# Sliding-window attention of a two-layer hybrid block: from token-major to feature-major output

## The reference

```python
scores = einsum('bnqhgd,bnkhd->bnhgqk', qb, k_ctx) * (A_HEAD_DIM ** -0.5)   # blocks of 128 queries
logits = where(valid, scores + bias, -inf)                                   # 128 or 256 keys per block
m = maximum(max(logits, axis=-1), sink)
p = exp(logits - m[..., None])
denom = sum(p, axis=-1) + exp(sink - m)
out = einsum('bnhgqk,bnkhd->bnqhgd', p / denom[..., None], v_ctx)            # S x 1024, 64 per head
...
y = sigmoid(ga) * (hm @ w_branch_m) + sigmoid(gb) * (ha @ w_branch_a)        # ha is out
```

## Time and profile before

| | |
|---|---|
| median of three executions | 2336.69 us |
| profiled execution | 2337.24 us, of which 2335.5 us are the span |
| TensorE matmul busy | 2273.0 us (97%) |
| VectorE, ScalarE, GpSimd busy | 921.2, 974.2, 886.1 us |
| mean granted TensorE clock | 0.990 of full speed |

### The profile page before, as it was taken

One profiled execution on the slowest core, in us unless ns is written; L12 is line 12 of the kernel. 1 busy time (PEld: TensorE's weight loads), 2 busy tenths in 40 slices (PEclk: granted clock), 3 DMA queues, 4 the chain that ended last, 5 costly groups with the idle time before them and its releaser, 6 DMA issues.

```text
span 2335.5 us, 35652 instructions
## 1 busy us (share of the span) xinstructions
PE 2273.0 (97%) x11333; PEld 1897.7 (81%) x11333; DVE 921.2 (39%) x1901; ACT 974.2 (42%) x2062; POOL 886.1 (38%) x672
## 2 busy tenths in 40 slices
PE   7999999999999999999999999999999999999996
PEld 5888888788888888888888788888888878888885
DVE  7344343423232235343343423232235535555452
ACT  5445455433232234455455434232235245445442
POOL 3332333445444444333323345444444231221213
PEclk9999999999999999999999999999999999999998
DMA  3221221223322222221212223323222320211112
GB/s 125 82 82 63 81 77 66 80 91 108 99 91 99 99 90 87 86 80 63 90 63 75 70 99 104 99 94 99 99 90 92 128 90 29 72 63 41 67 36 72
DMA packets 58793, 193.84 MB, mean 83 GB/s; under 512 B 6654, under 2 KB 11311, under 8 KB 58352
## 3 DMA queue, kind: packets, MB, share of 16 engines
q1 hardware_dynamic: 50400, 177.48, 22.5%
q10 hardware_dynamic: 8336, 15.60, 1.9%
HBM read 190.89 MB, written 2.16 MB: 83 GB/s over the span
## 4 chain that ended last, share of the span: by engine, by line
PE 92%; DVE 4%; ACT 2%; issue 1%; ACTq 0%; DVEq 0%; POOL 0%; POOLq 0%
PE ps L486 25%; PE ps L488 25%; PE ps L487 25%; PE ps L548 5%; PE ps L528 3%; PE ps L536 3%; PE ps L647 1%; PE ps L502 1%; PE ps L635 1%; PE ps L752 1%; PE ps L813 1%; DVE nt L1469 0%; PE ps L802 0%; PE ps L625 0%; DVE sz L1401 0%
## 5 line engine op out<-in xcount | busy, mean ns | idle before, releaser
L447 POOL TENSOR_TENSOR w_lo<-w_raw,w_hi 128x512 fp32r<-128x512 f32 x664 | 879.6, 1328 | 1428.7 <-ACT w_hi L863 1424.9
L486 PE MATMUL ps<-hT_hi,w_hi 128*128 128x512 f32 x1600 | 650.6, 407 | 2.5 <-DVE x2v L1361 2.0
L488 PE MATMUL ps<-hT_hi,w_lo 128*128 128x512 f32 x1600 | 628.1, 393 | 0.0
L487 PE MATMUL ps<-hT_lo,w_hi 128*128 128x512 f32 x1600 | 626.2, 391 | 0.0
L863 ACT ACTIVATE w_hi<-w_raw 128x512 fp32r<-128x512 f32 x664 | 411.4, 626 | 476.4 <-PE ps L488 446.8
L486 PEld LDWEIGHTS ps<-hT_hi,w_hi 128*128 128x128 f32 x1600 | 302.9, 189 | 65.8 <-issue 8.3
L488 PEld LDWEIGHTS ps<-hT_hi,w_lo 128*128 128x128 f32 x1600 | 301.8, 189 | 66.0
L487 PEld LDWEIGHTS ps<-hT_lo,w_hi 128*128 128x128 f32 x1600 | 303.0, 189 | 55.7 <-issue 0.5
L486 PE MATMUL ps<-u_hi,w_hi 128*128 128x512 f32 x512 | 199.2, 389 | 0.0
L487 PE MATMUL ps<-u_lo,w_hi 128*128 128x512 f32 x512 | 199.2, 389 | 0.0
L488 PE MATMUL ps<-u_hi,w_lo 128*128 128x512 f32 x512 | 199.2, 389 | 0.0
(11 more groups left out here) (289 smaller groups left out, 3269.7 us busy)
## 6 DMA issues: line engine op xcount, KB each, us to landing
w_raw<-w_all SPq DMA_DIRECT2D x332, 512.0 KB, 3.2
bias<-scr_w ACTq DMA_DIRECT2D x8, 512.0 KB, 3.8
biasn<-scr_n ACTq DMA_DIRECT2D x4, 1024.0 KB, 5.2
w1k<-w_in ACTq DMA_DIRECT2D x2, 1024.0 KB, 7.7
w1v<-w_in ACTq DMA_DIRECT2D x1, 2048.0 KB, 13.7
out<-x SPq DMA_DIRECT2D x8, 256.0 KB, 2.0
x<-x_in SPq DMA_DIRECT2D x4, 256.0 KB, 6.1
x<-x_in ACTq DMA_DIRECT2D x4, 256.0 KB, 5.7
```

Source lines behind the costliest of these rows:

```text
L447: nc.gpsimd.tensor_tensor(w_lo[:, h, :], raw[:, h // 2, (h % 2) * HALF:(h % 2 + 1) * HALF], w_hi[:, h, :].bitcast(F32), ALU.subtract).then ...
L486: nc.tensor.matmul(ps[:, p, :], wh, hi[:, kk, :], start=(kk == 0), stop=False)
L487: nc.tensor.matmul(ps[:, p, :], wh, lo[:, kk, :], start=False, stop=False)
L488: last = nc.tensor.matmul(ps[:, p, :], wl, hi[:, kk, :], start=False, stop=(kk == KT - 1))
```

## The change

The window attention of the head loop is rewritten (`WINDOW`, with steps `WS`, `wscale`, `WT`, `WV`, `wsum`).

- `WS` takes two heads: four score matmuls into one bank, two minima on VectorE, two exps on ScalarE. The sink's logit stands in one extra column of `L`, ahead of the scores, so that the exp's row sum is the whole denominator (129 or 257 columns). The probabilities of the four heads of a query tile go to `Pw` (two buffers).
- `wscale`: VectorE takes the reciprocal of the four sums and multiplies each head's probabilities by it, in place.
- `WT`: four transposes (four heads, one key tile) into one bank, 128x512. ScalarE rounds them to fp32r (high part), VectorE subtracts for the low part (`PTw`, two buffers), and that frees the bank. The first `WT` of a pass does so in two halves in two banks.
- `WV`: the stationary operand is `v_hl`, the high and the low part of the values side by side (64 + 64 columns); the high, then the low part of the probabilities of four heads move, 512 columns each, all fp32r.
- `wsum`: PSUM rows 0 to 63 hold the part of the values' high half, rows 64 to 127 that of the low half. ScalarE copies the first to `ohalf`, VectorE adds the two (two instructions, 64x256) and writes `ha32`, which is now feature-major at once.
- `ostat`, `otail`, `TA` and their waits are gone. `hnorm` 0 gains a subtraction for the values' low part ahead of the one for the keys, and a small copy. The 15 gate quarters in this stretch stay 15, at new places.

```diff
+WINDOW = [
+    ("WS", 0, 0), ("WS", 0, 1), F, ("hnorm", 1), ("WS", 1, 0), F, ("WS", 1, 1), ("wscale", 0), F, ("hnorm", 2), ("WT", 0, 0), F,
+    ("WS", 2, 0), F, ("wscale", 1), ("WV", 0, 0), ("WS", 2, 1), F, ("WT", 1, 0), ("wsum", 0), ("WT", 1, 1), F,
+    ("TH", 0), ("WS", 3, 0), F, ("wscale", 2), ("WV", 1, 0), ("WV", 1, 1), ("WS", 3, 1), F, ("WT", 2, 0), ("wsum", 1), ("WT", 2, 1), F,
+    ("TH", 1), F, ("wscale", 3), ("WV", 2, 0), ("WV", 2, 1), F, ("WT", 3, 0), ("WT", 3, 1), F, ("wsum", 2), F, F,
+    ("WV", 3, 0), ("WV", 3, 1), ("wsum", 3)]
...
# TensorE
+                        elif s[0] == "WT":
+                            qt, c = s[1], s[2]
+                            pe.wait_ge(scaled, I * TT + qt + 1)
+                            for n, t in enumerate(us):
+                                pe.wait_ge(t_free[t.b], t.m + 1)
...
+                        elif s[0] == "WV":
...
+                            for t in cur["WT", qt, c]:
+                                pe.wait_ge(t_free[t.b], t.m + 2)
+                            slot = PTw[window_slot(qt, c) % 2]
+                            nc.tensor.matmul(ps[:, 6 + ob, :], v_hl[:, k0 + c, :], slot[:, 0, :], start=(c == 0), stop=False)
+                            last = nc.tensor.matmul(ps[:, 6 + ob, :], v_hl[:, k0 + c, :], slot[:, 1, :], start=False,
+                                                    stop=(c == nk - 1))
...
# ScalarE
-                        elif s[0] == "TA":
-                            act.wait_ge(t_ready[us[0].b], us[0].m + 1)
-                            nc.scalar.activation(ha32[:, 2 * it + s[1], :], ps[:, 4 + us[0].b, :], ACT.Copy)\
-                                .then_inc(t_free[us[0].b], 1)
...
+                        elif s[0] == "WT":
+                            slot = window_slot(s[1], s[2])
+                            act.wait_ge(pv_used, I * 7 + slot + 1)
+                            for n, t in enumerate(us):
+                                part = slice(0, S) if len(us) == 1 else slice(2 * n * P, 2 * (n + 1) * P)
+                                act.wait_ge(t_ready[t.b], t.m + 1)
+                                nc.scalar.activation(PTw[slot % 2][:, 0, part], ps[:, 4 + t.b, part], ACT.Copy).then_inc(pt_hi, 1)
...
# VectorE
                             dve.wait_ge(staged_a, I + 1)
                             dve.wait_ge(s_free[cur["ST"].b], cur["ST"].m + 2)
+                            V.tensor_tensor(v_hl[:, :, DH:2 * DH], vtok[:, it, :, :], v_hl[:, :, 0:DH].bitcast(F32), ALU.subtract)
                             V.tensor_tensor(kg_lo[:, :], kdup[:, it, :], kg_hi[:, :].bitcast(F32), ALU.subtract)\
                                 .then_inc(k_lo, 1)
+                            V.tensor_copy(L[:, :, W0 - 1:W0], st[:, 11, 0:GH].unsqueeze(2))
...
+                        elif s[0] == "wscale":
+                            qt, n = s[1], min(s[1] + 1, 2) * P
+                            dve.wait_ge(probs, I * 16 + qt * GH + GH)
+                            link(V.reciprocal(st[:, 5, qt * GH:(qt + 1) * GH], st[:, 1, qt * GH:(qt + 1) * GH]))
+                            for hd in range(GH):
+                                p_ = Pw[:, qt % 2, hd, W0:W0 + n]
+                                last = V.tensor_scalar(p_, p_, st[:, 5, qt * GH + hd:qt * GH + hd + 1], None, ALU.mult)
+                            last.then_inc(scaled, 1)
+                        elif s[0] == "WT":
...
+                                V.tensor_tensor(PTw[slot % 2][:, 1, part], ps[:, 4 + t.b, part],
+                                                PTw[slot % 2][:, 0, part].bitcast(F32), ALU.subtract).then_inc(t_free[t.b], 1)
```

More of the change, by code:

```diff
@@ L52 @@
 VIT, VL, VN = 20, 18, 24
+W0 = 4
+WROW = W0 + 2 * P
 def unit(kind, n):
@@ L149, in takes, with window_slot @@
         out.append("e")
-    return out
+    if step == ("WT", 0, 0):
+        out.append("T")
+    if step[0] == "WV" and step[2] == 0:
+        out.append(f"O{step[1] % 2}")
+    return out
+def window_slot(qt, c):
+    return (2 * qt - 1 + c if qt else 0)
 def per(steps):
@@ L295, in two_layers_and_nsa @@
         sigmo = new("sigmo", [P, 2, S], at=a)
+        L = new("L", [P, GH, WROW], at=[a[0]])
         cv = new("cv", [P, S], at=a)
         vtmp = new("vtmp", [P, 2, S], at=a)
-        junk = vtmp[:, 0, 0:MDV]
+        junk = vtmp[:, 1, MDV:2 * MDV]
+        ohalf = new("ohalf", [P, S], at=[a[0]])
         negM = new("negM", [MH, S], at=a)
@@ L655, in _ @@
                                 pe.wait_ge(k_lo, I + 1)
-                                cur["Om"] = [w.next("O0"), w.next("O1")]
-                            attend(s, us, aq, (kg_hi, kg_lo), vg, I, False, I * 16)
+                            pe.wait_ge(s_free[b_], us[0].m + 1)
+                            k0 = max(qt - 1, 0)
+                            n = (qt + 1 - k0) * P
+                            for e in range(2):
+                                for i in range(2):
+                                    last = nc.tensor.matmul(ps[:, 2 + b_, e * n:(e + 1) * n],
+                                                            aq[:, 2 * pr + e, qt * P:(qt + 1) * P],
+                                                            (kg_hi, kg_lo)[i][:, k0 * P:k0 * P + n], start=(i == 0), stop=(i == 1))
@@ new lines, in _ @@
+                            last.then_inc(s_ready[b_], 1)
+                        elif s[0] == "WT":
[3 more added lines that the diff above has]
+                                pe.wait_ge(t_free[t.b], t.m + 1)
+                                heads = range(GH) if len(us) == 1 else range(2 * n, 2 * n + 2)
+                                for hd in heads:
+                                    last = nc.tensor.transpose(ps[:, 4 + t.b, hd * P:(hd + 1) * P],
+                                                               Pw[:, qt % 2, hd, W0 + c * P:W0 + (c + 1) * P], ident[:, :])
+                                last.then_inc(t_ready[t.b], 1)
+                            cur["WT", qt, c] = us
+                        elif s[0] == "WV":
+                            qt, c = s[1], s[2]
+                            k0, nk, ob = max(qt - 1, 0), min(qt + 1, 2), qt % 2
+                            if c == 0:
+                                pe.wait_ge(o_free[ob], us[0].m + 1)
+                            for t in cur["WT", qt, c]:
[4 more added lines that the diff above has]
+                                                    stop=(c == nk - 1))
+                            last.then_inc(pv_used, 1)
@@ L1168, in _ @@
                     act.wait_ge(t_free[b_], w.next("T", b_) + 1)
-                for src, dst in ((hm32, hm_hl[0]), (ha32, ha_hl[0])):
+                    act.wait_ge(o_free[b_], w.next(f"O{b_}") + 1)
+                for src, dst in ((hm32[:, :, :], hm_hl[0]), (ha32[:, :, :, :].rearrange("p g n s -> p (g n) s"), ha_hl[0])):
                     for k in range(KT):
```

107 lines of the change are left out of this document (59 added, 48 removed), and 2 rows, old and new, of the table TAKES.

## The result

The changed kernel takes 2350.57 us (median of five, 2347.82 to 2351.67), the kernel before 2337.32 in the same comparison: ratio 1.0059, 95% interval 1.0048 to 1.0069. It is slower by 13.3 us, outside the forecast's own range of 2331 to 2347 and inside the wide one of 2318 to 2352. The profiled execution took 2350.57 us, span 2348.8. Of all the executions behind this document one stands apart, in e3: it took 4545.84 us, nearly twice the others; the ratio given there leaves it out, and its cause was not followed.

The account below looks back on a forecast made before the run. TensorE, busy 97%, bounds the kernel. A pass: 31.5 + 4.9 of waits + 0.45 = 36.8 us against 36.56, +2 in eight, plus twice 0.3 at loop ends: 2339 us; own range 2331 to 2347, wide 2318 to 2352.

Parts of the forecast that it names:

- TensorE without waits: Rewritten stretch of one head pass: TensorE's issue alone takes 31.5 us, 5.1 less than before with waits.
- wait before `WT` 0, 0: TensorE waits 1.3 us for the scaling of tile 0, queued on VectorE behind the minima of `WS` 1, 1.
- wait before `WV` 0, 0: TensorE waits 1.2 us for subtractions queued behind ScalarE's tanh and VectorE's sigmoid, `hnorm` 2 and scalings.
- waits before `TH` 0 and `TH` 1: TensorE waits 0.8 and 1.0 us for banks that VectorE's queue frees late.
- wait before `WT` 3, 0: TensorE waits 0.5 us for the scalings of tile 3, behind a sigmoid that waits for a tanh.
- `kg_lo` later: In `hnorm` 0 the values' subtraction ahead of the keys' one adds 0.45 us a pass to the path.
- wait at a loop's end: TensorE's wait for the first `hm_lo`: some 3.2 us instead of 2.87, +0.3, twice.
- The product's pace of 0.23: The 14 new products with the values run at a gate matmul's 0.229 us; at 0.3 the kernel takes 2347 us.
- second rival: VectorE slower than the rows taken, at scalings of `Pw` and subtractions: 1.6 us more a pass, 2352 us; 17%.
- waits 2 and 4: Before `WV` 0, 0 1.2 us; before `WT` 3, 0 0.5 us and `WT` 1, 0 0.1 us.
- first rival: Queues less full than walked: half of the pass's waits go, 2.4 us instead of 4.9, 2319 us; 27%.
- third rival: The granted clock falls once a pass behind the new waits, 1.4 us each, +11 us: 2350 us; 9%.

Follow-up runs that it names:

- e3: Changed kernel with `WV` 3, 0, `WV` 3, 1 and `wsum` 3 moved ahead of the pass's last gate quarter: 2345.07 us, ratio 1.0033.
- e10: Changed kernel with another order of `WINDOW` and the keys' subtraction ahead of the values' one in `hnorm` 0: 2296.19 us, ratio 0.9824.
- e1: GpSimd's subtraction making `w_lo` cut from 512 to 64 columns, in both kernels: changed kernel 2322.21 us, kernel before 2325.92 us.
- e2: Changed kernel with the scaling of tile 0 ahead of the scores and minima of `WS` 1, 1: 2357.0 us, ratio 1.0082.
- e7: Changed kernel in its own order, without the sixteen multiplications of `Pw` by the reciprocals: 2337.08 us, ratio 1.0002.
- e9: As e8, with VectorE multiplying the probabilities once more, by 1.0, ahead of each scaling (16 more instructions): 2338.75 us, ratio 1.0012.
- e4: Changed kernel, same instructions, another order of `WINDOW`: VectorE-fed steps at least one gate quarter later behind their subtraction or scaling: 2305.02 us.
- e11: Changed kernel with a third new order of `WINDOW` and the keys' subtraction first in `hnorm` 0: 2298.28 us, ratio 0.9838.
- e8: Changed kernel in the order of e4, keys' subtraction first in `hnorm` 0, `TH` 1 ahead of `WS` 3, 1: 2306.27 us, ratio 0.9868.

## Why the prediction was half right

The forecast was 2339 us, the result 2350.6: it foresaw that the gain would be handed back as waits, but not that more would be handed back than was gained. The sum's own steps, each against what was measured in the first pass (waits from start to start, as the walk counted them):

| step | forecast | measured |
|---|---|---|
| TensorE without waits | 31.5 | 31.6 (36.56 − 5.0, e10) |
| wait before `WT` 0, 0 | 1.3 | 1.32 |
| wait before `WV` 0, 0 | 1.2 | 1.72, in e1 0.96 less |
| waits before `TH` 0 and `TH` 1 | 1.8 | 1.1 |
| wait before `WT` 3, 0 | 0.5 | 1.40, in e1 0.96 less |
| `kg_lo` later | 0.45 | 0.34 (0.52 − 0.18) |
| wait at a loop's end | +0.3 each | +0.62 each |

The measured rows of the stretch, without that of `kg_lo`, add up to 37.1 of its 37.47 us; the other 0.3 was not followed. The waits were 5.5 us instead of 4.9, and this small difference hides larger ones of both signs: +1.4 us at `WV` 0, 0 and `WT` 3, 0, −0.7 at the two `TH`.

- **TensorE's issue** was right to 0.1 us, and "the gain on TensorE is handed back as waits" is what happened. e10 shows 5.0 of the 5.1 us a pass that I said it would bring if nothing waited. The product's pace of 0.23, which I had left inside the second rival, was right too.
- **The failed term** is the price of the scalings and of `hnorm` 2 in waits 2 and 4. I priced each instruction by its duration or pace alone: "four scalings 1.05", "a scaling of 256 columns 0.26". What GpSimd was doing beside them was not in the walk. e1 takes it away, and 0.96 us goes from each of the two waits. With these off the five waits are 3.6 us (1.32 + 1.72 + 1.1 + 1.40 − 1.92), and my 4.9 would have been too high, not too low.
- **The rows had it.** In the earlier trace rows L1655, an operation on 128x4 elements, takes 613 ns, where L1648 on the same size takes 178. I took the 0.62 into the sum as that instruction's price. It is a held instruction too, and in the changed kernel (there L1708) it takes 156 ns: the hold passed from it to the scaling behind it and grew. Its row in the kernel before, and in the kernel before with the short subtraction (there L1658):

```profile
L1655 DVE TENSOR_TENSOR st<-st x8: 606/612/616, 121.7 to 1276.0; 128x4 f32<-128x4 f32 x8
```

```profile
L1658 DVE TENSOR_TENSOR st<-st x8: 156/157/157, 117.3 to 1267.7; 128x4 f32<-128x4 f32 x8
```

- The keys' 943 ns was the same: in the changed kernel, where the values' subtraction takes the hold first, the keys' takes 0.68, as it does in the kernel before with the short subtraction. The second rival took the 0.94 against 0.69 as the price of operands in SBUF; it was the hold. The subtraction that I added at "0.42 to 0.47" cost 0.34.
- **The end of a loop**: +0.62 instead of +0.3 each (3.49 against 2.87). "The clock's half-speed stretch stays" was wrong in the profiled run: 6.8 us of it instead of the 3.4 of the earlier trace rows behind layer 0's loop. Passes 9.3 and the two waits 1.2 make 10.5 of the 13.3 us; that stretch, at half speed, can account for 1.7 more. The rest is not followed.
- **The first rival** (fewer waits) had the right place and the wrong reason. Half of the waits do go, but only in another order.
- **The second rival** (2352, 17%) named VectorE's queue and the operations all in SBUF. It was nearest to the truth and had the wrong form: not 0.1 us more on each instruction, but up to 1 us on the one that meets GpSimd. That the result lies inside the wide range is owed to this rival's 2352 us, so in part to luck. It should have had the larger chance.
- **The third rival** did not occur: the waits of 1.55 us left the clock at 1.00 in all eight passes. e2, e7 and e9 show it behind waits of 2.25 to 2.89 us, where it cost mostly 0.7 to 1.7 us a pass. The Trainium skill ("TensorE: Matmul & The Clock Gate", "A second HAM failure mode: psum-queue depth-cycling") warns of this; by these traces it applies here behind the longer waits and not behind the shorter.

## What to carry to other kernels

Before pricing an instruction by a row, compare its duration with its size, with its own minimum and with another of the same size: one that is too long for its elements may have been held, and the question is by whom. The minimum alone doesn't tell it where the hold comes every time (L1655: 606 to 616 ns). A wait that is removed from an in-order queue is won only if the next wait isn't fed by the same chain: here one was moved in full (e2), and most of the gain came when the producers were moved together, a gate quarter or more ahead of their readers (e4, e10). Then a hold is harmless too (e11). A busy share of 42% says nothing of the slack of a queue: 16 more instructions on VectorE, in the order of e8, cost 32 us (2.8 us in a pass, and falls of the clock besides).

## What the runs showed of the hardware

- VectorE's scalings and subtractions with all operands in SBUF, where they start behind a GpSimd subtraction, don't end before that one does: 1369 ns instead of 342 for 128x256, 612 instead of 157 for 128x4, 1346 instead of 693 for 128x512 (e3). Instructions with a PSUM source were not held: in e8 a minimum takes its usual 0.47 us at 134.43, beside a GpSimd subtraction from 133.87 to 135.16. It goes the other way too. In the changed kernel a GpSimd subtraction that starts at 434.21, inside a run of eight of VectorE's `ha_lo` subtractions, takes 2.51 us instead of 1.28. The Trainium skill ("SBUF — State Buffer", "Who interferes with whom") describes an exclusive lock on a port pair shared by the two engines: between GpSimd and a VectorE operation in a 2-port mode, whoever issues first has the pair for the whole instruction, and an operation with two SBUF inputs contends with a GpSimd instruction that reads SBUF. The trace agrees, as far as one goes by the page for which kind an instruction is: the scalings (1369 against 342 ns) would be of the first, L1655 (612 against 157) is of the second.
- It is a sum of places, not a rate: with GpSimd's work at 64 columns a pass gained 0.45 us in the kernel before and 2.2 in the changed one, though GpSimd's work was the same in both. e10 has all of GpSimd's work, and none of its scalings was held.
- A fall of the granted clock from 1.00 to 0.50 inside a pass cost mostly 0.7 to 1.7 us (1.95 us in one pass of e2, 2.9 in one of e9), and it did not come in every pass with the same wait: of the six passes measured from one `negM` matmul to the next, two ran without a fall in e2, two in e7 and one in e9.
